# Sixteen experts of the first unit found and released in two halves, the query product moved one output product forward, the result stored by token tile

## The reference, cut to what matters

```python
x = layer_norm(DEEPNORM_ALPHA * x + mix, ln1_g[l], ln1_b[l])
ffn = peer(x, peer_wq[l], peer_subkeys[l], peer_u[l], peer_v[l])
x = layer_norm(DEEPNORM_ALPHA * x + ffn, ln2_g[l], ln2_b[l])

# in peer, for each token and each of 8 heads
s1, i1 = lax.top_k(sc[:, :, 0], PEER_TOPK)            # 16 of 128 keys
s2, i2 = lax.top_k(sc[:, :, 1], PEER_TOPK)
cand = (s1[..., :, None] + s2[..., None, :])          # 256 pairs
top_s, top_c = lax.top_k(cand, PEER_TOPK)             # 16 experts of 16384
e = i1[top_c // 16] * N_KEYS + i2[top_c % 16]
g = softmax(top_s)
act = gelu(einsum('cd,ced->ce', xc, peer_u[e]))
out = einsum('ce,ced->cd', g * act, peer_v[e])
```

## Time and profile before

| what | value |
|---|---|
| median of 3 runs | 3602.16 us (3597.86 to 3607.34) |
| the profiled execution | 3606.05 us, its span 3604.3 us |
| mean granted TensorE clock | 0.962 of full |
| PE busy | 3276.6 us, 91% |
| DVE, ACT, POOL busy | 1673.5, 704.6, 600.7 us |
| gathers, q0 | 536.90 MB in 73728 packets |

### The profile page before, as it was taken

The page is one execution under the profiler, slowest core; times in us unless marked ns, Lnnn a source line. Parts: engine busy times, 40 slices in busy tenths (PEclk is TensorE's granted clock), DMA queues, the critical chain, the costliest instruction groups (busy, mean ns, idle before and its releaser), DMA issues. The chain is left out here.

```text
span 3604.3 us, 46867 instructions
## 1 busy us (share of the span) xinstructions
PE 3276.6 (91%) x16986; PEld 2323.2 (64%) x16986; DVE 1673.5 (46%) x4191; ACT 704.6 (20%) x1581; POOL 600.7 (17%) x516
## 2 busy tenths in 40 slices
PE   8999789999989999999998888887899988888877
PEld 7887377878867888886887433443378873334433
DVE  2113541111146552111446777777514467777775
ACT  2100311101012121100232222222202322222222
POOL 0000000000000000000002544444200024444443
PEclk9999689999999989999999999999999999999999
DMA  4443013343423003434336999999843379999998
GB/s 182 149 157 130 0 48 118 147 160 139 152 91 118 14 3 140 172 124 158 133 137 279 421 421 422 422 422 421 342 152 137 122 289 421 421 422 422 422 422 337
DMA packets 113624, 827.95 MB, mean 230 GB/s; under 512 B 12528, under 2 KB 14064, under 8 KB 15120
## 3 DMA queue, kind: packets, MB, share of 16 engines
q0 software_dynamic: 73728, 536.90, 35.8%
q1 hardware_dynamic: 37184, 273.59, 20.3%
q10 hardware_dynamic: 2576, 15.59, 1.3%
HBM read 824.99 MB, written 1.05 MB: 229 GB/s over the span
## 5 line engine op out<-in xcount | busy, mean ns | idle before, releaser
L2671 PE MATMUL psum_all<-expert_rows,const_sb 128*128 128x512 f32 x2048 | 965.9, 628 | 205.9 <-ACT const_sb L2583 205.7
L2270 POOL DMA_INDIRECT expert_rows<-in_peer_uv_dram,head_experts x512 | 600.5, 1173 | 2960.1 <-issue 2405.7
L2671 PEld LDWEIGHTS psum_all<-expert_rows,const_sb 128*128 128x128 f32 x2048 | 401.1, 200 | 753.0 <-issue 466.1
L278 PE MATMUL psum_all<-xn,weight_ring 128*128 128x272 f32 (+1 forms) x3456 | 784.9, 390 | 14.6 <-DMA weight_ring<-in_ffn_in_dram 11.4
L278 PEld LDWEIGHTS psum_all<-xn,weight_ring 128*128 128x128 f32 x3456 | 658.4, 191 | 139.9 <-DMA weight_ring<-in_ffn_in_dram 9.5
L2422 DVE CUSTOM_DVE_ANT_0 expert_rows<-expert_rows,xn 128x1024 f32<-128x1024 f32 x512 | 617.4, 1223 | 281.0 <-DMA expert_rows<-in_peer_uv_dram,head_experts 276.8
L278 PE MATMUL psum_all<-hidden,weight_ring 128*128 128x272 f32 (+1 forms) x1408 | 318.6, 389 | 0.0
L278 PEld LDWEIGHTS psum_all<-hidden,weight_ring 128*128 128x128 f32 x1408 | 267.5, 190 | 50.5
L1926 PE MATMUL psum_all<-x,weight_ring 128*128 128x256 f32 x1024 | 228.6, 381 | 0.0
L2583 ACT ACTIVATE const_sb<-cst,head_weights 128x128 f32<-128x128 f32 x496 | 158.6, 390 | 336.6 <-DVE head_weights L2433 334.4
L1926 PEld LDWEIGHTS psum_all<-x,weight_ring 128*128 128x128 f32 x1024 | 191.7, 190 | 28.8 <-issue 3.5
(11 more groups left out here) (501 smaller groups left out, 3162.8 us busy)
## 6 DMA issues: line engine op xcount, KB each, us to landing
weight_ring<-in_ffn_in_dram SPq DMA_DIRECT2D x88, 1024.0 KB, 4.8
weight_ring<-in_w_in_dram SPq DMA_DIRECT2D x48, 1024.0 KB, 4.9
weight_ring<-in_ffn_out_dram SPq DMA_DIRECT2D x32, 1408.0 KB, 6.2
weight_ring<-in_hyb_in_dram SPq DMA_DIRECT2D x12, 1024.0 KB, 4.8
weight_ring<-in_peer_q_dram SPq DMA_DIRECT2D x12, 1024.0 KB, 9.6
expert_rows<-in_w_v_dram ACTq DMA_DIRECT2D x8, 1024.0 KB, 6.5
weight_ring<-in_br_attn_dram SPq DMA_DIRECT2D x8, 1024.0 KB, 6.8
weight_ring<-in_br_lru_dram SPq DMA_DIRECT2D x8, 1024.0 KB, 5.8
```

Source lines behind the costliest of these rows:

```text
L278: mm = pe.matmul(banks[s * halves + h], wt[:, h, k, :], rhs[:, k, :], start=(k == 0), stop=(k == ktiles - 1))
L2270: pool.indirect_dma_start(out=rows[:, j, :], out_offset=None, in_=a["peer_uv"], in_offset=bass.IndirectOffsetOnAxis(ap=idx[:, n, j:j + 1], ...
L2671: mm = pe.matmul(sums(n, half), diag[:, j, :], rows[:, j, D + half * 512:D + (half + 1) * 512], start=False, stop=last and j == TOPK - 1)
```

## The change

DVE gets a search of its own for unit (0,0), `find_first_experts`, in the place of `find_best` and `find_experts`: it takes the best eight pairs, turns them into expert numbers and signals `found`, and then does the same for the next eight. POOL waits for `found` before slot 0 and before slot 8; every other unit signals twice at once. On PE `first_query(0)` stands behind `out_product(9)` instead of `out_product(10)`. On DVE `add_out(10)` goes behind the first keys and `add_out(11)` behind the whole search. Each tile of the result is stored by a transfer of its own, inside the layer's phase, and the phase that stored it is gone.

```diff
@@ SP
-                            sp.wait_ge(S.found, QT * PH)
+                            sp.wait_ge(S.found, 2 * QT * PH)
...
+                        else:
+                            for n in range(QT):
+                                sp.wait_ge(tile_out[n], KD)
+                                sp.dma_start(out[:, :, n * P:(n + 1) * P], h[:, :, n * P:(n + 1) * P]).then_inc(S.stored, 16)
+                            sp.wait_ge(S.stored, 16 * QT)
@@ POOL
-                                pool.wait_ge(S.found, u + 1)
-                                pool.sem_inc(S.held, 1)
                                 for j in range(TOPK):
+                                    if j % (TOPK // 2) == 0:
+                                        pool.wait_ge(S.found, 2 * u + j // (TOPK // 2) + 1)
+                                        pool.sem_inc(S.held, 1)
@@ DVE
-                            dve.sem_inc(S.found, 1)
+                            dve.sem_inc(S.found, 2)
+
+                        def find_first_experts():
+
+                            for part in (slice(0, 8), slice(8, TOPK)):
+                                if part.start:
+                                    held(dve.match_replace(cand, best[:, 0:8], cand, -3e38))
+                                held(dve.max(best[:, part], cand))
+                                held(dve.max_index(besti[:, part], best[:, part], cand))
+                                dve.tensor_scalar(pos[:, 0, part], besti[:, part], 4, None, ALU.logical_shift_right)
+                                step(dve.tensor_scalar(pos[:, 1, part], besti[:, part], 15, None, ALU.bitwise_and))
+                                step(dve.tensor_copy(posf[:, :, part], pos[:, :, part]))
+                                cube = [P, 2, TOPK // 2, TOPK]
+                                step(dve.tensor_tensor(hot[:, :, part, :], posf[:, :, part].unsqueeze(3).to_broadcast(cube),
+                                                       iota.unsqueeze(1).unsqueeze(1).to_broadcast(cube), ALU.is_equal))
+                                step(dve.tensor_tensor(hot[:, :, part, :], hot[:, :, part, :], topf[:, :, :].unsqueeze(2).to_broadcast(cube), ALU.mult))
+                                step(dve.tensor_reduce(pick[:, :, part], hot[:, :, part, :], AX, ALU.add))
+                                step(dve.scalar_tensor_tensor(out=pick[:, 0, part], in0=pick[:, 0, part], scalar=float(NKEYS), in1=pick[:, 1, part],
+                                                              op0=ALU.mult, op1=ALU.add))
+                                step(dve.tensor_scalar(idx[:, 0, part], pick[:, 0, part], vec2("expert_base"), None, ALU.add))
+                                dve.sem_inc(S.found, 1)
...
                         add_out(KD + 1)
+                        find_first_keys(0, 0)
                         add_out(KD + 2)
-                        find_first_keys(0, 0)
-                        add_out(KD + 3)
-                        for piece in pieces[1:]:
-                            piece(0, 0)
+                        find_pairs(0, 0)
+                        find_first_experts()
                         shift(0)
-                        for t in range(KD + 4, 2 * KD):
+                        for t in range(KD + 3, 2 * KD):
                             add_out(t)
@@ PE
-                        for t in range(KD, KD + 3):
+                        for t in range(KD, KD + 2):
                             out_product(t)
                         pe.wait_ge(heads_in, 16 * 2)
                         first_query(0)
                         pe.wait_ge(S.keys_in, 16)
                         first_scores(0)
+                        out_product(KD + 2)
                         out_product(KD + 3)
@@ after the layer loop
-        with phase(nc, "stored") as (block, S):
-            @block.sync
-            def _(sp):
-                sp.dma_start(out, h).then_inc(S.stored, 16)
-                sp.wait_ge(S.stored, 16)
```

More of the change, by code:

```diff
@@ L1755, in constants2, with second_block @@
     return c
-def second_block(nc, a, w, h, scaled, spare, cst, psum, psum_all):
+def second_block(nc, a, out, w, h, scaled, spare, cst, psum, psum_all):
     with ExitStack() as ctx:
@@ L2236, in second_block @@
                 with phase(nc, *names, "held", "dve_held", "found", "slot_free", "dotted", "gelus", "weights_ready", "diagonals", "shifted", "exps",
-                           "keys_in", "query_ready", "query_in", "key_products", "scores_in", "x_turned", "x_in", "out_turned", "out_in",
+                           "keys_in", "query_ready", "query_in", "key_products", "scores_in", "x_turned", "x_in", "out_turned", "out_0", "out_1", "stored",
                            "ln_sums", "variance", "root", "ln_scaled", "normed", "first_query", "first_in", "first_scores", "first_keyed",
@@ L2242, in second_block @@
                     head_in = (S.head_in_0, S.head_in_1, S.head_in_2)
+                    tile_out = (S.out_0, S.out_1)
                     first = S.index(S.landed_0)
@@ L2506, in out_gain @@
                             for k in range(4):
-                                dve.tensor_scalar(h[:, k, n * P:(n + 1) * P], late_turn(n, k), vec2("ln2_g", k, 1), vec2("ln2_b", k, 1), ALU.mult, ALU.add).then_inc(S.out_in, 1)
+                                dve.tensor_scalar(h[:, k, n * P:(n + 1) * P], late_turn(n, k), vec2("ln2_g", k, 1), vec2("ln2_b", k, 1), ALU.mult, ALU.add).then_inc(tile_out[n], 1)
                         def first_tile_out(b):
@@ L2520, in _ @@
                         out_gain(1)
-                        dve.wait_ge(S.out_in, 2 * QT * 4)
+                        for n in range(QT):
+                            dve.wait_ge(tile_out[n], KD)
                     @block.scalar
@@ L2554, in out_gain @@
                             for k in range(4, KD):
-                                act.activation(h[:, k, n * P:(n + 1) * P], late_turn(n, k), ACT.Identity, bias=vec2("ln2_b", k, 1), scale=vec2("ln2_g", k, 1)).then_inc(S.out_in, 1)
+                                act.activation(h[:, k, n * P:(n + 1) * P], late_turn(n, k), ACT.Identity, bias=vec2("ln2_b", k, 1), scale=vec2("ln2_g", k, 1)).then_inc(tile_out[n], 1)
                         def single(hd, n):
@@ L2912, in program @@
         spare = xn[:, :, :].rearrange("p k t -> p (k t)")[:, 0:QT * D]
-        second_block(nc, a, w, h, xn[:, :, META:], spare, (kept[:, :], None), psum, psum_all)
-        with phase(nc, "stored") as (block, S):
-            @block.sync
-            def _(sp):
-                sp.dma_start(out, h).then_inc(S.stored, 16)
-                sp.wait_ge(S.stored, 16)
+        second_block(nc, a, out, w, h, xn[:, :, META:], spare, (kept[:, :], None), psum, psum_all)
 def kernel(**inputs):
```

## The result

| | before | changed |
|---|---|---|
| median of 15 runs each | 3602.16 us | 3610.53 us |
| range | 3597.86 to 3607.34 | 3606.12 to 3618.88 |
| span of the profiled execution | 3604.3 us | 3612.9 us |

The change costs 8.4 us: the ratio of changed to before is 1.0022, 95% interval 1.0015 to 1.0028. The two spans differ by 8.6 us, so the profile can account for it.

The account below looks back on a forecast made before the run. Transfer engines are full once gathers start, so the latency chain before the first gather counts. Savings of 2 x 3.50 + 1.45 = 8.45 us take 3602.16 to 3593.7 us, range 3588.5 to 3599.5.

Parts of the forecast that it names:

- The query, moved: PE's query ahead of the last output product starts 0.87 us earlier, not the whole 1.84, as ACT's normed piece limits it.
- The search in two halves: DVE's split search saves 2.63 us before the first found; with the query, the first gather comes 3.50 us earlier.
- rival on layer 1's start: Something other than found sets layer 1's first gather: up to 2.04 us lost, 3595.7 (3597.2 with all gone); chance 0.10.
- The price of issuing while DVE searches: POOL's first gather issued during DVE's search could cost 0 to 1.05 us a layer; taken as 0.
- What becomes late: PE's product 15 waits for the late addition; tile 1 comes 4.1 to 5.6 us late, unit (0,1) found 1.8 to 3.3 later.
- Does the stream run dry?: Gather stream before unit (0,1): of 7.5 us of cover, 0.7 to 2.2 remain, so no cost.
- The store: Storing each tile separately at the program's end saves 1.45 us net, bounds 2.25 saved to 1.6 lost.
- Slower: Rival: unit (0,1)'s search sets the pace, a loss from 8.2 us of lateness in both layers; 3605.7 at 10 us; chance 0.04.

Follow-up runs that it names:

- late_add: Kernel before, with only product 11's addition moved behind the search and its shift: 3603.24 us, ratio 0.9998.
- later_sums: late_add with 16 more matmuls on PE in front of tile 1's sums: 3616.71 us (one run).
- narrow: Changed kernel with every gather cut from 8 KB to 2 KB of a row; no time given, wait ended 20.1 and 20.0 us after the first gather.
- held_until_sums: Changed kernel with slots 7 to 13 given to GpSimd only after PE waits for tile 1's sums' semaphore: 3596.38 us, ratio 0.9978.
- add_early_held: Changed kernel with product 11 added before the search halves and slots 7 to 13 held until tile 1's sums' semaphore: 3592.72 us, ratio 0.9980.
- store_only: Kernel before with only the store by token tile added: 3602.80 us, ratio 0.9998.
- eight_behind: Changed kernel with product 11 added before the search halves and eight more matmuls behind tile 1's sums: 3603.52 us, ratio 0.9997.
- pe_busy: Changed kernel with 48 more matmuls on PE behind tile 1's sums: 3599.08 us (one run).
- dve_busy: Changed kernel with 24 small operations on DVE in front of centre(1): 3603.45 us (one run).
- row_of_four: Changed kernel with product 11 added before the halves, four gathers before tile 1's sums' semaphore and the other ten behind it: 3595.35 us, ratio 0.9972.
- dve_fourteen: Changed kernel with 14 small operations on DVE in front of centre(1): 3600.47 us (one run).

## Why the prediction was wrong, step by step

- **The query, moved.** Said 0.87 earlier; 0.86 in layer 2. Right.
- **The search in two halves.** Said: first gather 3.50 earlier. It is 3.65 and 3.78 earlier. Right. In layer 1 the distance between `found` and the gather stayed at 3.2 us, so the rival on layer 1's start falls. The price of issuing while DVE searches was 0: the gathers of layer 2's row take 0.94 each, as alone.
- **What becomes late.** This is the step that failed: "1.84 for product 15, 0.30, those 1.13, and the 2.98 from 2935.66 to `centre(1)` at 2938.64: 2942.75, 4.1 us late", up to 5.6. PE's part of it was near: the sums ended 5.5 and 5.7 us later than before, against the begin of the output products. But from the sums to `centre(1)` I carried over the 0.03 us of before, when they ended 0.2 and 2.2 us after the first gather. Now they end 9.3 and 11.6 us into an unbroken row of gathers, and it was 10.5 and 8.2: a wait that the sum put at nothing, without a row that showed it at such a place. Unit (0,1) was found 11.5 and 12.0 us later, not 1.8 to 3.3. late_add prices the lateness alone, with the increment in time and on a chip where nothing was held: 0.4 and 3.3 us, no change of the time.
- **Does the stream run dry?** The arithmetic was right and its input wrong: 7.5 us of cover less 3.5 is 4.0, and 11.5 to 12.0 less 4.0 is 7.5 to 8.0 a layer, measured as 7.5 us without data in layer 2. The spans' +8.6 is made of 4.35 and 4.16 in the two layers (each some -3.7 of the earlier start, which leaves 7.9 to 8.0 of dry stream), 1.1 in front of the output products, which the change doesn't touch, and -1.0 at the end, where the store's -1.87 stands against 0.9 for the last transposes (1.97 us at a granted clock of 0.50 instead of 1.09 at 1.00).
- **The store.** Said -1.45; -1.87. A little more than I said, and no sign of the small packets in the way of the last gathers.
- **The rivals.** "Slower" was the right mechanism in kind: unit (0,1)'s search sets the pace from 8.2 us of lateness on. It had 0.04 because I looked for the missing 5 us in PE's clock and "a second wait on top", which I had no row for. For 12 us its own formula gives 3602.2 + 2 x 4.5 - 1.45 = 3609.8; measured 3610.5.

**What is shown.** In the changed kernel the sums' semaphore came 10.5 and 8.2 us late, and the dry stream that followed accounts for the loss. On chips where this happens it goes with the length of POOL's row (seven, ten, fourteen gathers: `centre(1)` at 10.1, 14.4 and 19.8 us after the first gather), it comes without the halves (later_sums), and it stays with a quarter of the bytes (narrow). Taken away on such a chip, the change is worth what was forecast: held_until_sums 0.9978, against 0.9977 in the forecast, and add_early_held 0.9980. And the order of the kernel before is struck too (store_only, by 8.4 us), only later in the chain, at the query instead of the sums, and there the cover takes it. What the change did wrong is to put the sums, and with them all of tile 1's norm, query and search, behind the point at which the hold-up ends.

**Open** is what holds the semaphore, and why it does so on some chips only, or at some times only: each batch is one chip at one time, so the two can't be told apart. In the traces that were hit, each semaphore of the sums or of the query that fell due 7.0 us or more into a row still going on came late, and those of the sums due at 4.7 us or earlier came within 1.1 us. But that of product 15, due at 7.4 us in layer 2 of the changed kernel, was in time, and so was that of the scores in layer 1 of store_only, due at 14.2. In the other seven traces those of the sums and the query were in time from 6.0 to 17.5 us into the row. A theory must explain both, the missing records and the spread-out matmuls of later_sums and eight_behind; I have none that does. Whether the changed kernel would be faster than before where nothing is held is untested as well: pe_sixteen is the changed order with 16 idle matmuls, in one run on chip 1, and took 3597.07 us against 3608.3 in one run of the kernel before.

The Trainium skill (SBUF — State Buffer, "Who interferes with whom") names the port pair of DVE and GpSimd as the only thing over which engines contend. In the changed kernel DVE stood idle for 12.19 us while POOL issued its gathers and PE's semaphore was late, so the rows here show another hold-up than that.

## What to carry to other kernels

When a reordering moves a hand-off between engines into a stretch in which GpSimd issues a long unbroken row of indirect gathers, the old latency of that hand-off is no guide: here it went from 0.03 us to between 8 and 13 in most of the runs that were hit. Where that happens, give GpSimd its slots in shorter rows until the last critical semaphore is through (one moved increment and a wait: -0.2% here on chip 14, against the +0.2% of the changed kernel), which costs nothing while the data in flight cover it. And in a profile, a wait put down to "remote" whose supposed releaser ended long before is a place to look at first. Before you call a remedy found, run the kernel without it on the same chip: here five remedies (pe_busy, dve_busy, row_of_four, dve_fourteen, pe_sixteen) were tried only where perhaps nothing needed one.

## What the runs showed of the hardware

- In 13 of 20 traces (the changed kernel's and all from chips 9, 14 and 5) a semaphore of TensorE's matmuls was 0.97 to 12.9 us late in or just behind a row of GpSimd's indirect gathers; in the other 7 none was. In the first 13 semaphore records are missing from the first row of gathers on, in the 7 none.
- Where it was held by a row of fourteen gathers, the sums' semaphore came 19.8 to 20.1 us after the first of them in all 15 layers, 2.2 to 2.9 us after the last gather's issue had ended. Behind ten it was 2.1 to 2.3 us, behind seven 1.6 to 1.7.
- The query's semaphore was held in the same way where the sums' had been in time, in four of five layers until 19.9 to 20.2 us after the first gather, once until 12.7.
- It was the same with 2 KB a row as with 8 KB.
- In one layer each, 16 matmul records in that row took 6.5 us instead of 1.95, and 32 took 9.5 instead of 5.2 to 6.7.
